# Mixture of experts: the low part of the second half of each w2 slab, made on GpSimd instead of VectorE

## The reference, cut to what matters

```
def moe_swiglu(x, router_w, router_b, w1, w3, w2):
    ...
    for e in range(N_EXPERTS):
        out = out + gate[..., e:e + 1] * swiglu(x, w1[e], w3[e], w2[e])
    return out

def swiglu(x, w1, w3, w2):
    return (jax.nn.silu(x @ w1) * (x @ w3)) @ w2
```

## Time and profile before

| | |
|---|---|
| three timed runs | 3278.77 us median, 3267.85 to 3280.75 |
| the profiled execution, its own time | 3269.48 us |
| its span in the profile | 3267.2 us |
| PE busy | 2916.1 us, 89% |
| DVE busy | 2074.1 us, 63% |
| ACT busy | 1531.9 us, 47% |
| POOL busy | 20.9 us, 1% |
| stage of the experts | about 881 to 1727 us of the span, 8 items |
| `lo` on DVE (L2175) | 528 instructions, 629.7 us, 1223 ns each |

### The profile page before, as it was taken

How to read it: one execution, slowest core, us unless ns; L and a number is a source line. 1 busy time by engine, 2 the same in 40 slices (tenths; PEclk the granted TensorE clock), 3 DMA queues, 4 the chain that set the end, 5 groups by cost and what they waited for, 6 DMA issues and landing times. The chain is left out here.

```text
span 3267.2 us, 45648 instructions
## 1 busy us (share of the span) xinstructions
PE 2916.1 (89%) x17630; PEld 2458.6 (75%) x17630; DVE 2074.1 (63%) x2925; ACT 1531.9 (47%) x2269; POOL 20.9 (1%) x22
## 2 busy tenths in 40 slices
PE   6788997978799999999996998869898998869898
PEld 5666886965677778777775888659787888659787
DVE  4453772445388888988883765574476775575466
ACT  3233332324277777877773434353343434353333
POOL 0000000010000000000000000000000000000000
PEclk9778998976899999999998999879999999879999
DMA  6401553300479888888864555215344555215351
GB/s 253 129 27 63 191 184 118 115 2 1 171 293 360 321 337 316 354 322 321 343 260 188 194 191 186 73 59 200 143 183 151 192 183 190 80 52 207 131 192 58
DMA packets 107516, 598.96 MB, mean 183 GB/s; under 512 B 26116, under 2 KB 34394, under 8 KB 38504
## 3 DMA queue, kind: packets, MB, share of 16 engines
q1 hardware_dynamic: 99288, 591.01, 48.4%
q10 hardware_dynamic: 8080, 5.89, 0.6%
HBM read 593.94 MB, written 6.12 MB: 184 GB/s over the span
## 5 line engine op out<-in xcount | busy, mean ns | idle before, releaser
L2175 DVE TENSOR_TENSOR expert_w_low<-weight_ring,expert_w_high 128x1024 fp32r<-128x1024 f32 x528 | 629.7, 1223 | 75.3 <-ACT expert_w_high L2122 64.7
L631 PE MATMUL psum<-hnT_parts,weight_high 128*128 128x512 f32 x1760 | 636.0, 403 | 22.7 <-DVE weight_low L679 22.7
L2122 ACT ACTIVATE expert_w_high<-weight_ring 128x1024 fp32r<-128x1024 f32 x528 | 552.6, 1058 | 95.8 <-PE psum L2051 54.2
L633 PE MATMUL psum<-hnT_parts,weight_low 128*128 128x256 f32 x1760 | 498.5, 283 | 0.0
L631 PEld LDWEIGHTS psum<-hnT_parts,weight_high 128*128 128x128 f32 x1760 | 336.0, 191 | 106.8 <-DVE weight_low L679 24.6
L679 DVE TENSOR_TENSOR weight_low<-weight_ring,weight_high 128x1024 fp32r<-128x1024 f32 x330 | 384.0, 1219 | 13.5 <-ACT weight_high L673 13.5
L481 PE MATMUL psum<-hnT_parts,slab_high 128*128 128x256 f32 x2016 | 371.5, 287 | 18.5 <-DVE slab_low L524 18.5
L633 PEld LDWEIGHTS psum<-hnT_parts,weight_low 128*128 128x128 f32 x1760 | 338.0, 192 | 3.9
L524 DVE TENSOR_TENSOR slab_low<-weight_ring,slab_high 128x2048 fp32r<-128x2048 f32 (+3 forms) x120 | 205.4, 1725 | 209.7 <-ACT slab_high L516 209.7
L481 PEld LDWEIGHTS psum<-hnT_parts,slab_high 128*128 128x128 f32 x2016 | 321.0, 196 | 20.5 <-DVE slab_low L524 20.5
L673 ACT ACTIVATE weight_high<-weight_ring 128x1024 fp32r<-128x1024 f32 x330 | 324.1, 1046 | 14.6 <-PE psum L645 8.3
(11 more groups left out here) (392 smaller groups left out, 4511.9 us busy)
## 6 DMA issues: line engine op xcount, KB each, us to landing
weight_ring<-in_moe_w SPq DMA_DIRECT2D x264, 1024.0 KB, 6.8
weight_ring<-in_w_in SPq DMA_DIRECT2D x52, 1024.0 KB, 6.1
weight_ring<-in_ffn_w_gate SPq DMA_DIRECT2D x44, 1024.0 KB, 4.8
weight_ring<-in_ffn_w_up SPq DMA_DIRECT2D x44, 1024.0 KB, 6.3
weight_ring<-in_ffn_w_down SPq DMA_DIRECT2D x44, 1024.0 KB, 4.8
weight_ring<-in_ffn_w SPq DMA_DIRECT2D x33, 1024.0 KB, 4.9
weight_ring<-in_w_gate SPq DMA_DIRECT2D x24, 1024.0 KB, 4.8
weight_ring<-in_w_branch SPq DMA_DIRECT2D x24, 512.0 KB, 3.5
```

Source lines behind the costliest of these rows:

```text
L631: nc.tensor.matmul(out, hi[:, kt, :], hn[2][:, kt, :, :], start=(kt == 0), stop=(kt == KT - 1), skip_group_check=True)
L633: last = nc.tensor.matmul(out[:, 0:SEQ], lo[:, kt, :], hn[0][:, kt, :], start=False, stop=(kt == KT - 1), skip_group_check=True)
L2122: nc.scalar.activation(part(0, k, half), raw(c, k, half), ACT.Copy).then_inc(high[k].sem, 1)
L2175: nc.vector.tensor_tensor(part(1, k, half), raw(c, k, half), as_f(part(0, k, half)), ALU.subtract).then_inc(low[k].sem, 1)
```

## The change

The `lo` of W2_1 is taken from VectorE and given to GpSimd, in a block of its own that waits for `hi` W2_1 and signals on a new semaphore, `low_w2_second`. `low[W2]` is now raised once for each chunk, by the `lo` of W2_0. TensorE's `down` waits for `low[W2]` before its half 0 and for the new semaphore before its half 1, and SyncE waits for both before it refills a w2 slab. Nothing else changes: the buffers, the slabs, and the orders of TensorE, ScalarE and SyncE are the same.

```diff
+        self.low_w2_second = sig("expert_low_w2_second")
...
+    PER = (2, 2, 1)
...
                     for k in range(3):
-                        sp.wait_ge(low[k].sem, done)
+                        sp.wait_ge(low[k].sem, done * PER[k])
+                        if k == W2:
+                            sp.wait_ge(M.low_w2_second.sem, done)
...
                     for j in range(2):
-                        t.wait_ge(low[W2].sem, i * 2 * CH + (2 * (CH + c) + j + 1))
+                        t.wait_ge((low[W2], M.low_w2_second)[j].sem, i * CH + (CH + c + 1))
...
+            @block.gpsimd
+            def _(g):
+                items = g.value_load(count_at, min_val=NE, max_val=MAX_ITEMS)
+                with g.Fori(0, items) as i:
+                    for c in range(CH):
+                        g.wait_ge(high[W2].sem, i * 2 * CH + (2 * c + 2))
+                        nc.gpsimd.tensor_tensor(part(1, W2, 1), raw(c, W2, 1), as_f(part(0, W2, 1)),
+                                                ALU.subtract).then_inc(M.low_w2_second.sem, 1)
...
-                    for k in range(3):
+                    for k in (UP_A, UP_B):
                         for half in range(2):
                             lo(0, k, half, i)
+                    lo(0, W2, 0, i)
...
                         if c:
-                            for half in range(2):
-                                lo(c, W2, half, i)
+                            lo(c, W2, 0, i)
```

More of the change, by code:

```diff
@@ L2007, in _ @@
                     for c in range(3, CH):
-                        loads(e, c, i * 2 * CH + 2 * (CH + c - 2))
+                        loads(e, c, i * CH + (CH + c - 2))
                     following = sp.value_load(table[0:1, bass.ds(i + 1, 1)], min_val=0, max_val=NE - 1)
                     for c in range(3):
-                        loads(following, c, i * 2 * CH + 2 * (CH + [9, 10, 8][c] + 1))
+                        loads(following, c, i * CH + (CH + [9, 10, 8][c] + 1))
                 e = sp.value_load(table[0:1, bass.ds(items - 1, 1)], min_val=0, max_val=NE - 1)
                 for c in range(3, CH):
-                    loads(e, c, items * 2 * CH + 2 * (c - 2))
+                    loads(e, c, items * CH + (c - 2))
                 for k in range(3):
-                    sp.wait_ge(low[k].sem, items * 2 * CH + 2 * CH)
+                    sp.wait_ge(low[k].sem, (items * CH + CH) * PER[k])
+                sp.wait_ge(M.low_w2_second.sem, items * CH + CH)
                 for n in range(W.next, W.next + SLOTS):
@@ L2026, in _ @@
                     t.sem_inc(used[k].sem, 2)
-                    t.sem_inc(low[k].sem, 2 * CH)
+                    t.sem_inc(low[k].sem, PER[k] * CH)
+                t.sem_inc(M.low_w2_second.sem, CH)
                 for b in range(2):
```

## The result

The changed kernel takes 3285.99 us (median of 10 runs) against 3272.03 us before (median of 10): ratio 1.0038, 95% interval 1.0024 to 1.0051, so 8 to 17 us slower. The forecast was +13 us and 3286 us.

The account below looks back on a forecast made before the run. TensorE was taken as the bound, busy 76.35 of 80 us, VectorE next. Terms 7.2 - 4.7 + 10.4 = +13 us gave 3282 by the profiled execution's 3269.5; with runs' median 3278.8 the forecast was 3286, range 3263 to 3320.

Parts of the forecast that it names:

- They take turns at 2.16 us: GpSimd and VectorE instructions using both SBUF ways exclude each other, each turn costing VectorE 2.16 us; chance 0.66.
- the wait at chunk 1: Item start: A0 of chunk 1 starts 1.03 us later behind GpSimd, TensorE with it; +7.2 us over seven items.
- not held: Rival: VectorE isn't held by GpSimd, or wins without a gap; the kernel gains 12.6 us; chance 0.2.
- the signs named ahead: Changed profile: GpSimd 2.3 to 2.5 us, A0 2 to 2.5, chunk 1 wait 2.6, no `add` waits, new `expert_hid_low` waits.
- a dearer GpSimd: Rival: GpSimd much slower on fp32r results, sign above 2.6 us; about +130 us at a cost of 4; chance 0.08.
- Iteration 1: `add` reads PSUM beside GpSimd and comes 1.14 us earlier, removing TensorE's mean wait of 0.59 us; -4.7 us in all.
- Iterations 2 to 9: VectorE's chain becomes longer than TensorE's 8.45 us a chunk; stalls of 1.3 us an item, +10.4 us in all.
- The chain of 8.58 us: Iterations 2 to 9: VectorE's five `lo` and two small ones, 6.42 us, plus GpSimd's turn of 2.16.
- the cover of 0.5 us at the first `down`: Iteration 2: `expert_hid_low` ends at 1234.1 before `down` at 1234.67; each iteration uses 0.13 to 0.16 of this.
- The stall at `weighed`: Iteration 4: `weighed` and `place`, 1.12 us, stand uncovered behind GpSimd; with 0.2 cover left, a stall of 0.9 us.
- The item's end, the refills: No cost: 1.5 us cover at the item's end; refills leave 1 to 2 us later, hidden by the ring.
- The sum: Experts' stage: item starts 7.2, iteration 1 -4.7, iterations 2 to 9 10.4, together +13 us; bounds +2 and +32.

Follow-up runs that it names:

- e3: Changed kernel with GpSimd subtracting only 4 columns and filling the other 1020 with zeros, so it writes but hardly reads; ratio 0.9967 to the kernel before.
- e4: Changed kernel with the low parts of both W2 halves on GpSimd, chunk 0's too; ratio 1.0191 to the kernel before.
- e2: Changed kernel with only chunk 1's subtraction on GpSimd, the other chunks' back on VectorE; ratio 0.9980 to the kernel before.
- e1: Changed kernel with only chunk 0's subtraction on GpSimd, the other ten of an item back on VectorE; ratio 1.0042 to the kernel before.
- e5: Changed kernel with chunk 0's subtraction back on VectorE, the other ten of an item on GpSimd; ratio 1.0003 to the kernel before.
- e6: Changed kernel with `weighed` and `place` made in iteration 1 instead of 4; ratio 1.0038 to the kernel before.
- e11: Changed kernel with chunk 0's subtraction back on VectorE and `weighed` and `place` in iteration 1; ratio 0.9986 to the kernel before.
- e7: Kernel before, without GpSimd, with chunk 0's two w2 halves moved behind chunk 1's first halves on ScalarE and VectorE; ratio 1.0044 to the kernel before.
- e8: Kernel before with chunk 0's w2 halves moved behind chunk 1's first halves, and chunk 1's subtraction alone on GpSimd; ratio 1.0078 to the kernel before.

## Why the prediction was right

- **They take turns at 2.16 us.** Right: 2.36 us for a free GpSimd subtraction (2.35 worked out), 2.13 us for a turn in VectorE's chain (8.55 - 6.42), and the wait at chunk 1 longer by 1.03 us, as predicted. e3 shows that without the reading `lo` isn't held, e4 that the cost grows with the dose, e2 that PSUM operands are free. The rival "not held" is out. It was given 0.2 partly because rows 8 were called a single meeting; the trace has a second one like it, where `X_and_XT` takes 1.31 us again, from 692.36. Of the signs named ahead, A0 is longer at chunk 1 than said (3.02 us, not 2 to 2.5), and GpSimd's records have a mean of 2.64 us, above the 2.6 that was to mean a dearer GpSimd. They contain its own waits for VectorE; free ones take 2.36. So no extra cost of the fp32r result is seen, though no run does the same subtraction with an f32 result.
- **Iteration 1.** Right in kind, mis-sized: -0.86 us an item, not -0.59. e2 shows the same 0.86 with this wait alone removed. The row gives TensorE's idle time, but from the first scatter product to the next `up` it took 3.86 us before (1216.26 to 1220.12) and 3.03 in e2 (1217.43 to 1220.46): 0.83 us, not 0.59.
- **Iterations 2 to 9.** The chain of 8.58 us was 8.55, the cover of 0.5 us at the first `down` 0.5 (1246.74 to 1247.27). The stall at `weighed` was mis-sized: I let all 1.12 us of `weighed` and `place` stand behind GpSimd's turn, but a part passes in it. From one `expert_hid_low` to the next it is 9.34 us there (1254.88 to 1264.22) and not 8.58 + 1.12 = 9.70, and 0.64 us were lost, not 0.9. The wait in the list is one of 0.47 us an item, where several from about 1 us on had been named as the sign. Altogether 1.0 us an item instead of 1.3.
- **The item's end, the refills.** Nothing there in the changed profile, as said. The 8 us by which its stage begins later than before weren't foreseen; with the same code ahead of it, e1, e3, e5, e6 and e11 begin at 881.6 to 886.3, around the 885.56 of before, so they aren't put down to the change.
- **The sum.** By these the change is 7 x 1.19 and 0.1 for the first item, 8.5 us, where I had 13. That is the size of the mechanism; it was overestimated by half.
- **Left out.** The falls of the clock at the longer wait: 1.6 us in the changed kernel's profile, which with 8.5 makes the 10.3 of the stage but for 0.2. That the other 2 us up to the ratio's 12.4 are more falls in the timed runs than in the profiled one is argued, not shown; the interval reaches down to 8 us. The forecast of +13 met +12 by luck in part: one term was too high and another missing. That 3286 met the median of 3285.99 is luck altogether, since it was set between two baselines, 3269.5 and the three runs' 3278.8, and ten runs of before have their median at 3272.0.

## What to carry to other kernels

Before elementwise work with two SBUF operands goes to an idle GpSimd, look at what VectorE has next in its queue: if that reads two tensors from SBUF, or one at the faster rate of `weighed`, each GpSimd instruction costs VectorE nearly its own whole length, here 2.13 us of 2.36, nearly twice the 1.13 that it saved; if it reads PSUM, the transfer was free here. A GpSimd instruction that only writes spared the first kind, and held the second. Place single instructions by that, since one of eleven decided the sign here. And a stall of TensorE's that is already there is a bad place to lengthen: it can cost clock besides.

## What I had not expected of the hardware

A wait of TensorE of 1.54 us at chunk 1, with one of 1.55 us 7 us ahead of it, left the clock at full in each of the items of before, e2, e5 and e11 behind the first. With about 2.57 us there it fell to 1.2 GHz in one of seven items of the changed kernel's profile, three of seven of e1's and three of seven of e6's, each fall worth some 1.3 to 1.6 us. The falls came between 0.4 us before TensorE began again and 0.9 us after. The other kernels fit in: none in e7 with its waits of 2.0 us, four of seven in e8 with 3.0 us, five of seven in e4 with 2.3 us (there worth only 0.6 us an item). A small wait can so cost 60% more than its length, in some items and executions and not in others; what decides between them is not shown.
